# Two x tiles get space of their own, and the orders of all engines are drawn up anew

## The chip, the cores and the metric

The kernel runs on one core of one Trainium2 chip. The metric is the device time of one execution in microseconds. The kernel before takes 1588.69 us, the median of three runs (1588.14 to 1590.66).

## What is computed

One hybrid layer on x of 2048 rows and 1024 columns: RMSNorm, a combined input projection, a sliding-window attention with 16 query and 4 key heads of 64, a retention with 8 heads of values of 128, gates by SiLU, the output projection and the residual. Of the reference, cut to what matters:

```python
h = rms_norm(x, norm_gain)
proj = jnp.einsum('bsd,de->bse', h, w_in)
aq, ak, av, ag, rq, rk, rv, rg = jnp.split(proj, SPLIT_POINTS, axis=-1)
attn = window_attention(aq, ak, av, q_norm_gain, k_norm_gain, sink_logits)   # window 128, ALiBi, sinks
ret = retention(rq, rk, rv, ret_norm_gain)        # chunks of 64, state carried, group norm
mixed = jnp.concatenate([attn * jax.nn.silu(ag), ret * jax.nn.silu(rg)], axis=-1)
x = x + jnp.einsum('bse,ed->bsd', mixed, w_out)
```

## The kernel before

The sequence is cut into 4 blocks of 512 rows, the heads into 4 groups. A unit n is one block with one group, so there are 16 units, 0 to 15, and units 0 to 3 are the first block. A block has four x tiles of 128 rows, t = 0 to 3.

Every matmul is done in three: each operand is split into a high half (written by a copy to fp32r) and a low half (what is left), and high by high, high by low and low by high are added up. ScalarE (ACT) writes the high halves, GpSimd (POOL) the low halves of the weights, VectorE (DVE) those of x. In units 0 to 3 the weights are split on the chip and both halves saved to DRAM; later units load the halves.

TensorE (PE) works on jobs. Job(n, j) is one bank of 512 columns: j 0 to 3 are q, k and v of the four row tiles (weight panel 0 of the unit), 4 and 5 the attention gate, 6 and 7 the retention's q and k (panel 1), 8 to 11 its v and gate (panel 2), 12 to 19 the output projection (panel 3). The output jobs of unit n run within unit n + 1. Panels take turns in two buffers, wH and wL. Between the jobs stand the small operations of PE: TQ (transposes of the normalised q and k, L1453), S_ (scores, L1463), PT and PV (transposed probabilities, and their product with v), A, I and MT (retention), XB (the row scales, spread over a tile, L1553).

The first panels go as follows. load(q) (L312) brings a quarter of a panel, two of its eight k slices, to a staging slot; q 0 to 3 are panel (0,0), 4 to 7 panel (0,1), 8 to 11 panel (0,2). There are three slots, and q = 3 lies in sx, which is free at the start. wh1(n,p,s) (L520) on ACT writes the high half of slice s, wl1 (L382) on POOL the low half. A job that is first in its panel waits for each slice's low half (s_wl, L1434). x_turned(0,t) (L261) loads tile t of the transposed x to xt, which has two halves: tile 2 waits until the low halves of tile 0 are done (s_xL of 8), tile 3 those of tile 1. xh (L706) and xl (L1149) write the high and low half of tile t, in four pieces of two slices, to hTH and hTL. Jobs 0 to 3 need the slices of their own tile only, jobs 4 to 7 those of all four. xsq sums the squares of a tile of x rows, xms_ and xpow make the row scale from them; qkv(0,t) on ACT takes the bank of job(0,t) and that scale, qk_stats and qk_norm on DVE (L927, L938) normalise it, with rpow on POOL between them.

On DVE, carry_in(0) (L908) waits for the attention constants, part1 and part2 (L964, L990) are the softmax of a tile, ptl and mix take probabilities and result further, kw_am, kwl_al, rvg, rupd and gna to gnb belong to the retention. The pair qn lies in the same space as obt, which mix uses.

All DMAs go out from SyncE (SP), in its order. It waits in order too: an instruction that waits holds all those behind it. save(q) (L213) stores a quarter of a split panel.

Every engine has its order written out as calls, unit by unit (POOL L434 to L515, ACT L718 to L885, DVE L1157 on, PE L1564 to L1674). Dependencies are semaphores. The head of SP's order, of DVE's and of PE's stand in the diff.

Of the kernel before, what the change touches and what calls it, by code (L numbers as in the profile page):

```python
# [94 lines left out]
def build(nc, x, norm_gain, q_gain, k_gain, sinks, ret_gain, xT, wp0, wp1, wp2, wp3, c_bias, c_ret, c_ident, out):  # L95
# [9 lines left out]
    with ExitStack() as ctx:  # L105
# [272 lines left out]
        def _(pool):  # L378
# [62 lines left out]
            ggm(0, 0); wl1(1, 0, 3); ggm(0, 1); wl1(1, 0, 4); mixl(0, 2); wl1(1, 0, 5); wl1(1, 0, 6)
            wl1(1, 0, 7); mixl(0, 3); gpow(0, 0); ggm(0, 2); wl1(0, 3, 0); wl1(0, 3, 1); wl1(0, 3, 2)
            wl1(0, 3, 3); gpow(0, 1); ggm(0, 3); wl1(0, 3, 4)

            rpow(1, 0); wl1(0, 3, 5); wl1(0, 3, 6); wl1(0, 3, 7); gpow(0, 2); rpow(1, 1); rpow(1, 2)
            wl1(1, 1, 0); gpow(0, 3); wl1(1, 1, 1); wl1(1, 1, 2); rpow(1, 3); wl1(1, 1, 3); wl1(1, 1, 4)
            wl1(1, 1, 5); wl1(1, 1, 6); wl1(1, 1, 7); wl1(1, 2, 0); wl1(1, 2, 1); wl1(1, 2, 2); wl1(1, 2, 3)
            wl1(1, 2, 4); wl1(1, 2, 5); wl1(1, 2, 6); wl1(1, 2, 7); mixl(1, 0); rql(1); mixl(1, 1); rkl(1)
            wl1(2, 0, 0); wl1(2, 0, 1); wl1(2, 0, 2); mixl(1, 2); wl1(2, 0, 3); ggm(1, 0); wl1(2, 0, 4)
            wl1(2, 0, 5); wl1(2, 0, 6); wl1(2, 0, 7); ggm(1, 1); mixl(1, 3); gpow(1, 0); ggm(1, 2); wl1(1, 3, 0)  # L450
            wl1(1, 3, 1); wl1(1, 3, 2); wl1(1, 3, 3); wl1(1, 3, 4); ggm(1, 3); gpow(1, 1); wl1(1, 3, 5)

            rpow(2, 0); wl1(1, 3, 6); rpow(2, 1); wl1(1, 3, 7); gpow(1, 2); rpow(2, 2); wl1(2, 1, 0)
# [1277 lines left out]
```

## Time and profile before

| | before |
|---|---|
| median of three runs | 1588.69 us |
| the profiled execution | 1589.65 us |
| its span | 1587.9 us |
| mean granted TensorE clock | 0.998 |
| PE busy | 1560.4 us, 98% |
| DVE, ACT, POOL busy | 1113.1, 853.2, 451.4 us |
| share of PE in the chain that ended last | 84% |

The profile is of one execution. Busy times say how long an engine had an instruction in work; matmuls overlap, so that a busy PE isn't PE at its peak. The wait of an engine is named by what released it.

### The profile page before, as it was taken

What the parts mean: (1) busy time and instruction counts of PE and PEld (TensorE: products, weight loads), DVE (VectorE), ACT (ScalarE), POOL (GpSimd) and SP (SyncE); (2) the same over time, 40 slices, a digit from 0 to 9 for tenths busy, and PEclk for the clock granted to TensorE, in tenths of its full rate; (3) what the DMA queues carried; (4) which work ended last, traced back from release to release, by engine and by line L of the source; (5) the groups of instructions that cost most, each with busy time, mean ns of one, the idle gap of its engine ahead of it and who ended that gap; (6) DMA issues with size and microseconds to landing.
All of it is one profiled execution on the core that took longest, in us unless ns stands there. A gap on an engine that the chain in (4) does not pass through costs nothing.

```text
span 1587.9 us, 24908 instructions
## 1 busy us (share of the span) xinstructions
PE 1560.4 (98%) x8120; PEld 1354.2 (85%) x8120; DVE 1113.1 (70%) x2934; ACT 853.2 (54%) x2421; POOL 451.4 (28%) x453
## 2 busy tenths in 40 slices
...
GB/s 260 330 315 280 175 345 186 285 208 178 323 256 166 188 146 188 186 209 145 186 215 225 247 128 195 205 99 247 168 159 282 148 197 189 149 179 156 154 207 54
DMA packets 123328, 323.66 MB, mean 204 GB/s; under 512 B 16832, under 2 KB 60224, under 8 KB 123200
## 3 DMA queue, kind: packets, MB, share of 16 engines
...
## 4 chain that ended last, share of the span: by engine, by line
PE 84%; DVE 9%; issue 3%; ACT 2%; DMA 1%; POOL 1%; SPq 0%; DVEq 0%; POOLq 0%; ACTq 0%
PE jb L1441 24%; PE jb L1443 24%; PE jb L1442 24%; PE ob L1500 2%; PE s L1476 2%; PE ptb L1485 2%; PE ob L1460 1%; PE s L1539 1%; DMA stage<-wp_dram 1%; PE s L1538 1%; DVE hTL L1153 1%; PE ab L1550 1%; DVE acc L1139 1%; PE s L1377 1%; DVE qS L955 1%
## 5 line engine op out<-in xcount | busy, mean ns | idle before, releaser
L1441 PE MATMUL jb<-wH,hTH 128*128 128x512 f32 (+1 forms) x1024 | 376.6, 368 | 9.4 <-POOL wL L387 9.4
L1442 PE MATMUL jb<-wL,hTH 128*128 128x512 f32 (+1 forms) x1024 | 372.6, 364 | 0.0
L1443 PE MATMUL jb<-wH,hTL 128*128 128x512 f32 (+1 forms) x1024 | 372.3, 364 | 0.0
L1441 PEld LDWEIGHTS jb<-wH,hTH 128*128 128x128 f32 x1024 | 193.3, 189 | 30.0 <-POOL wL L387 11.9
L1443 PEld LDWEIGHTS jb<-wH,hTL 128*128 128x128 f32 x1024 | 193.3, 189 | 20.5
L1442 PEld LDWEIGHTS jb<-wL,hTH 128*128 128x128 f32 x1024 | 193.7, 189 | 17.6
L1441 PE MATMUL jb<-wH,mxH 128*128 128x512 f32 x512 | 207.6, 405 | 0.0
L1441 PE MATMUL jb<-hTH,wH 128*128 128x512 f32 x512 | 202.7, 396 | 2.8 <-POOL wL L387 2.8
L1443 PE MATMUL jb<-wH,mxL 128*128 128x512 f32 x512 | 200.6, 392 | 0.0
L1442 PE MATMUL jb<-wL,mxH 128*128 128x512 f32 x512 | 200.3, 391 | 0.0
L1442 PE MATMUL jb<-hTL,wH 128*128 128x512 f32 x512 | 199.7, 390 | 0.0
L1443 PE MATMUL jb<-hTH,wL 128*128 128x512 f32 x512 | 199.5, 390 | 0.0
L589 ACT ACTIVATE sx<-sx,nm 128x128 f32<-128x128 f32 x256 | 99.9, 391 | 160.9 <-DVE d L988 160.7
L412 POOL TENSOR_TENSOR mxL<-mixr,mxH 128x256 fp32r<-128x256 f32 x64 | 47.8, 747 | 465.4 <-ACT mxH L651 464.3
L387 POOL TENSOR_TENSOR wL<-stage,wH 128x512 fp32r<-128x512 f32 (+1 forms) x126 | 156.5, 1265 | 68.3 <-ACT wH L531 68.0
L1441 PEld LDWEIGHTS jb<-hTH,wH 128*128 128x128 f32 x512 | 96.2, 188 | 22.9 <-POOL wL L387 4.5
L1443 PEld LDWEIGHTS jb<-wH,mxL 128*128 128x128 f32 x512 | 96.1, 188 | 21.0
L1443 PEld LDWEIGHTS jb<-hTH,wL 128*128 128x128 f32 x512 | 96.1, 188 | 20.7
L1442 PEld LDWEIGHTS jb<-hTL,wH 128*128 128x128 f32 x512 | 96.3, 188 | 18.1
L1442 PEld LDWEIGHTS jb<-wL,mxH 128*128 128x128 f32 x512 | 96.6, 189 | 16.5
L1441 PEld LDWEIGHTS jb<-wH,mxH 128*128 128x128 f32 x512 | 96.3, 188 | 16.5
L394 POOL TENSOR_TENSOR rstd<-ms,mhalf 128x5 f32<-128x5 f32 x64 | 75.9, 1186 | 113.6 <-DVE ms L932 113.5
...
## 6 DMA issues: line engine op xcount, KB each, us to landing
...
```

What stands on the lines that cost most here:

```text
L387: pool.tensor_tensor(wL[b][:, s, 0:w], stage_of(at // 2, w)[:, s % 2], wH[b][:, s, 0:w].bitcast(F32), ALU.subtract).then_inc(S["s_wl"], 1)
L394: pool.tensor_tensor(rstd[:, t % 2], ms[:, t % 2], mhalf[:, 0:5], ALU.pow).then_inc(S["s_rstd"], 1)
L412: pool.tensor_tensor(mxL[:, 0:2, cols], mixr[:, :, :], mxH[:, 0:2, cols].bitcast(F32), ALU.subtract).then_inc(S["s_mixl"], 1)
L589: act.activation(v, v, ACT.Exp, bias=nm4[:, t % 2, i:i + 1], accum_out=den[:, t % 2, i:i + 1])
L955: v.scalar_tensor_tensor(out=qS[other, t % 2, :, a * 64:a * 64 + 64], in0=tr[rows, 0:256].rearrange("p (c q) -> p c q", q=64), scalar=qkg[ ...
L1139: v.tensor_tensor(a, a, bank_of(n, J_OUT + i)[:, :], ALU.add).then_inc(S["s_acc"], 1)
L1441: pe.matmul(o, lh, rh_, start=i == 0, stop=False)
L1442: pe.matmul(o, lh, rl_, start=False, stop=False)
L1443: m = pe.matmul(o, ll, rh_, start=False, stop=i == last)
L1476: m = pe.matmul(s_parts[:, par, hp], qS[:, t % 2, 2 * hp + par], kHL[:, :, win], start=True, stop=True)
L1485: m = pe.transpose(ptb[:, i * P:(i + 1) * P], sx[:, at:at + P], ident[:, :])
L1500: m = pe.matmul(o, v, pT[:, par * 256:(par + 1) * 256].rearrange("p (r q) -> p r q", q=64), start=i == 0, stop=i == 1)
```

## The change

A tensor xt23, two tiles of x in size, is declared in the space that mxL takes afterwards (mxL is now declared ahead of mxH, so that the two spaces are the same). Tiles 2 and 3 of the first block are loaded there, with no wait, with two semaphores of their own; ACT's and DVE's splits of them read from there. The condition for load(6) becomes that slot 0 is free of q = 0 (2 low halves, not 8). On SP, loads 6 and 4 go ahead of x tile 3, of the gains and of the attention constants, and load 5 ahead of the x rows of tile 2. qk_norm of the first two tiles of a unit waits until mix of the unit before has ended.

The orders of POOL, ACT, DVE and PE are new in all 16 units; much in units 0 to 4, by neighbours that change places in most others. In unit 0, PE has jobs 0 to 3 with nothing between them, TQ(0,0) behind job 4 and S_(0,0) behind job 5, and PV(0,3) goes to unit 1. ACT has the high halves of x tile 3 and four weight slices of panel 1 ahead of qkv(0,0); DVE has half of the low halves of x tile 3 behind qk_stats(0,0). From unit 5 on PE has "job(n,1); job(n,2); I(n-1,3)" everywhere. The core of the diff:

```diff
-        mxH, mxL = sb("mxH", [P, 4, BLK], F32R), sb("mxL", [P, 4, BLK], F32R)
+        with nc.sbuf_tensor("xt23", [P, 2, KT, P], F32) as xt23:
+            pass
+        mxL, mxH = sb("mxL", [P, 4, BLK], F32R), sb("mxH", [P, 4, BLK], F32R)
...
+        def x_tile(b, t):
+            return xt23[:, t - 2] if b == 0 and t >= 2 else xt[:, t % 2]
...
-                if t >= 2:
+                if b and t >= 2:
                     sp.wait_ge(S["s_xL"], 32 * b + 8 * (t - 1))
                 elif b:
                     sp.wait_ge(S["s_xsq"], nth(b, 4, t + 2))
-                sp.dma_start(xt[:, t % 2], xT[b, t]).then_inc(s_xt[t % 2], 16)
+                landed = s_xu[t % 2] if b == 0 and t >= 2 else s_xt[t % 2]
+                sp.dma_start(x_tile(b, t), xT[b, t]).then_inc(landed, 16)
...
-                if q >= STAGES + 1:
-                    sp.wait_ge(S["s_wl"], 2 * (q - STAGES) + 2)
+                if q > STAGES:
+                    sp.wait_ge(S["s_wl"], 2 * (0 if q == 6 else q - STAGES) + 2)
...
             first_rows(1)
+            load(6)
+            load(4)
             x_turned(0, 3)
             qk_gains()
             attention_constants(0)
-            load(4)
+            load(5)
             first_rows(2)
-            load(5)
             first_rows(3)
-            load(6)
             load(7)
...
+            xh(0, 0, 0); wh1(0, 0, 0); wh1(0, 0, 1); wh1(0, 0, 2); wh1(0, 0, 3); xh(0, 0, 1); wh1(0, 0, 4)
+            wh1(0, 0, 5); xh(0, 0, 2); wh1(0, 0, 6); wh1(0, 0, 7); xh(0, 0, 3); xh(0, 1, 0); xh(0, 1, 1)
+            xh(0, 1, 2); xh(0, 1, 3); xsq(0, 0); xh(0, 2, 0); xh(0, 2, 1); xh(0, 2, 2); xh(0, 2, 3); xsq(0, 1)
+            wh1(0, 1, 0); wh1(0, 1, 1); xh(0, 3, 0); xh(0, 3, 1); xh(0, 3, 2); xh(0, 3, 3); wh1(0, 1, 2)
+            wh1(0, 1, 3)
+
+            qkv(0, 0); wh1(0, 1, 4); wh1(0, 1, 5); xsq(0, 2); wh1(0, 1, 6); xsq(0, 3); qkv(0, 1); wh1(0, 1, 7)
+            xrb_copy(0); v_shift(0, 0); qkv(0, 2); v_shift(0, 1); qkv(0, 3); v_shift(0, 2); tqh(0, 0)
+            wh1(0, 2, 0); wh1(0, 2, 1); ag(0, 0); wh1(0, 2, 2); v_shift(0, 3); tqh(0, 1); wh1(0, 2, 3); ag(0, 1)
...
+                elif n:
+                    v.wait_ge(S["s_mixr"], 4 * n)
                 v.wait_ge(S["s_rstd"], nth(n, 4, t))
...
-            xms_(0, 0); xl(0, 1, 3); xl(0, 2, 0); xl(0, 2, 1); xl(0, 2, 2); xms_(0, 1); xl(0, 2, 3)
+            xl(0, 1, 3); xl(0, 2, 0); xl(0, 2, 1); xl(0, 2, 2); xms_(0, 0); xl(0, 2, 3); xms_(0, 1); carry_in(0)
+            xl(0, 3, 0); xl(0, 3, 1)
...
+            qk_stats(0, 0); xms_(0, 2); xl(0, 3, 2); xms_(0, 3); xl(0, 3, 3); qk_norm(0, 0); qk_stats(0, 1)
+            v_parts(0, 0); v_parts(0, 1); qk_norm(0, 1); qk_stats(0, 2); v_parts(0, 2); agz(0, 0)
+            qk_stats(0, 3); qk_norm(0, 2); tql(0, 0); agg(0, 0); v_parts(0, 3); agz(0, 1); qk_norm(0, 3)
+            tql(0, 1); agg(0, 1); part1(0, 0); rl(0, 0); rq_decay(0); tql(0, 2); part1(0, 1); part2(0, 0)
...
-            job(0, 0); job(0, 1); job(0, 2); TQ(0, 0); job(0, 3); S_(0, 0); job(0, 4); TQ(0, 1); XB(0)
-            job(0, 5); S_(0, 1); TQ(0, 2); job(0, 6); S_(0, 2); TQ(0, 3); PT(0, 0); job(0, 7); S_(0, 3)
-            PV(0, 0); PT(0, 1); job(0, 8); PV(0, 1); PT(0, 2); A(0, 0); job(0, 9); PV(0, 2); PT(0, 3); A(0, 1)
-            job(0, 10); PV(0, 3); I(0, 0); A(0, 2); job(0, 11); I(0, 1); A(0, 3)
+            job(0, 0); job(0, 1); job(0, 2); job(0, 3); XB(0); job(0, 4); TQ(0, 0); job(0, 5); TQ(0, 1)
+            S_(0, 0); job(0, 6); TQ(0, 2); S_(0, 1); job(0, 7); TQ(0, 3); S_(0, 2); job(0, 8); PT(0, 0); A(0, 0)
+            job(0, 9); PT(0, 1); S_(0, 3); PV(0, 0); A(0, 1); job(0, 10); I(0, 0); PT(0, 2); PV(0, 1); A(0, 2)
+            job(0, 11); I(0, 1); PT(0, 3); PV(0, 2); A(0, 3)
...
-            job(9, 0); I(8, 2); MT(8, 0); job(9, 1); I(8, 3); job(9, 2); TQ(9, 0); MT(8, 1); job(9, 3)
+            job(9, 0); I(8, 2); MT(8, 0); job(9, 1); job(9, 2); I(8, 3); TQ(9, 0); MT(8, 1); job(9, 3)
...
-            job(15, 0); I(14, 2); MT(14, 0); job(15, 1); I(14, 3); MT(14, 1); job(15, 2); TQ(15, 0); job(15, 3)
+            job(15, 0); I(14, 2); MT(14, 0); job(15, 1); job(15, 2); MT(14, 1); I(14, 3); TQ(15, 0); job(15, 3)
```

## Rows read from the trace of the kernel before

**Rows 1.** The page: busy us of PE, its share, its instructions.

```profile
PE 1560.4 (98%) x8120; PEld 1354.2 (85%) x8120; DVE 1113.1 (70%) x2934; ACT 853.2 (54%) x2421; POOL 451.4 (28%) x453
```

**Rows 2.** Table by stretches: busy us (count) of each engine, clock, DMA share, GB/s.

```profile
16.00:24.30 8.30, 8.30 (x49) 8.00 (x47) 4.36 (x20) 6.92 (x21) 2.76 (x3) 1.00 0.44 141
24.30:27.00 2.70, 0.42 (x3) 0.40 (x3) 1.55 (x9) 0.00 (x0) 0.00 (x0) 0.90 0.94 329
27.00:33.30 6.30, 6.29 (x31) 5.97 (x30) 3.24 (x13) 6.00 (x13) 5.11 (x5) 0.77 0.90 318
33.30:43.00 9.70, 6.90 (x29) 4.45 (x28) 9.17 (x20) 8.49 (x26) 9.14 (x8) 1.00 1.04 391
```

**Rows 3.** PE's waits, 0 to 100 us (total, times, longest), then its timeline.

```profile
PE jb L1441 <- POOL wL L387: 12.2, 9, 8.1
PE ob L1460 <- DVE rawqn L946: 2.3, 1, 2.3
PE ob L1500 <- DVE mixr L1028: 1.2, 1, 1.2
PE s L1476 <- DVE kHL L960: 1.0, 1, 1.0
...
32.83 0.74 PE L1476 MATMUL s<-kHL,qS 128*128 128x256 f32 x4
33.40 0.39 PE L1441 MATMUL jb<-hTH,wH 128*128 128x512 f32 x1
...
49.05 0.64 PE L1476 MATMUL s<-kHL,qS 128*128 128x256 f32 x4
...
96.69 0.34 PE L1441 MATMUL jb<-wH,hTH 128*128 128x384 f32 x1
```

**Rows 4.** Timelines of SP's queue, DVE and ACT: start, length, what, [idle before].

```profile
13.30 0.33 SPq L267 DMA_DIRECT2D xt<-xT_dram  x1
17.09 0.33 SPq L267 DMA_DIRECT2D xt<-xT_dram  x1
21.94 0.59 SPq L317 DMA_DIRECT2D stage<-wp_dram  x1
31.44 0.82 SPq L218 DMA_DIRECT2D scrH<-wH  x1
...
25.45 0.17 DVE L915 TENSOR_SCALAR nsink<-sink 128x2 f32<-128x2 f32 x1 [3.74 <-DMA sink<-sink_logits_dram]
...
27.19 1.15 ACT L531 ACTIVATE wH<-stage 128x512 fp32r<-128x512 f32 x2 [3.71 <-DMA stage<-wp_dram]
```

**Rows 5.** Timelines of POOL and DVE.

```profile
7.06 6.06 POOL L387 TENSOR_TENSOR wL<-stage,wH 128x384 fp32r<-128x384 f32 x6 [6.22 <-ACT wH L531]
...
73.86 1.20 POOL L412 TENSOR_TENSOR mxL<-mixr,mxH 128x256 fp32r<-128x256 f32 x1 [2.63 <-ACT mxH L651]
...
7.65 8.71 DVE L1153 SCALAR_TENSOR_TENSOR hTL<-xt,ngain,hTH 128x128 fp32r<-128x128 f32 x12 [1.43 <-ACT hTH L715]
...
16.46 2.31 DVE L1153 SCALAR_TENSOR_TENSOR hTL<-xt,ngain,hTH 128x128 fp32r<-128x128 f32 x8
```

**Rows 6.** The stretch from 33.3 to 97 us, and DVE's timeline.

```profile
33.30:97.00 63.70, 57.72 (x292) 46.69 (x291) 53.60 (x111) 42.23 (x118) 40.47 (x37) 1.00 0.90 325
...
37.04 1.30 DVE L986 SCALAR_TENSOR_TENSOR nm<-m,nsink 128x4 f32<-128x4 f32 x1
```

**Rows 7.** PE's waits from 100 to 1500 us, and from 1500 us to the end.

```profile
PE s L1538 <- issue: 2.2, 9, 0.3
PE ob L1460 <- DVE kHL L960: 1.7, 3, 0.7
PE ob L1500 <- DVE pTL L899: 0.8, 2, 0.6
PE ob L1500 <- DVE mixr L1028: 0.5, 1, 0.5
...
PE s L1538 <- DVE kwL L899: 1.1, 1, 1.1
```

More of the change, by code:

```diff
@@ L441, in _ @@
[L441 to L453, printed above, removed]
@@ new lines, in _ @@
+            gnm(0, 3); tql(1, 0); qk_stats(1, 3); gnb(0, 3); v_parts(1, 2); add(0, 0); qk_norm(1, 3); mtl(0, 2)
+            tql(1, 1); add(0, 1); v_parts(1, 3); add(0, 2); rl(1, 0); add(0, 3); tql(1, 2); mtl(0, 3)
+            part1(1, 0); add(0, 4); part1(1, 1); add(0, 5); tql(1, 3); add(0, 6); part2(1, 0); add(0, 7)
+            part2(1, 1); carry_out(1); agz(1, 0); part1(1, 2); ptl(1, 0); agg(1, 0); agz(1, 1); part2(1, 2)
+            ptl(1, 1); agg(1, 1); part1(1, 3); mix(1, 0); rq_decay(1); part2(1, 3); mix(1, 1); ptl(1, 2)
@@ new lines, in _ @@
+            qk_stats(2, 1); gnm(1, 2); v_parts(2, 1); gnb(1, 2); qk_norm(2, 1); gna(1, 3); gnv(1, 3)
+            qk_stats(2, 2); v_parts(2, 2); gnm(1, 3); mtl(1, 1); qk_norm(2, 2); gnb(1, 3); tql(2, 0)
+            qk_stats(2, 3); add(1, 0); v_parts(2, 3); add(1, 1); qk_norm(2, 3); mtl(1, 2); tql(2, 1); add(1, 2)
+            part1(2, 0); add(1, 3); tql(2, 2); mtl(1, 3); rl(2, 0); part1(2, 1); add(1, 4); part2(2, 0)
+            add(1, 5); xms_(1, 0); xms_(1, 1); xms_(1, 2); part2(2, 1); ptl(2, 0); tql(2, 3); add(1, 6)
@@ L1252, in _ @@
+            qk_stats(7, 2); v_parts(7, 2); tql(7, 0); gna(6, 3); gnv(6, 3); qk_norm(7, 2); mtl(6, 1); gnm(6, 3)
+            qk_stats(7, 3); v_parts(7, 3); gnb(6, 3); qk_norm(7, 3); add(6, 0); tql(7, 1); rl(7, 0); add(6, 1)
             part1(7, 0); mtl(6, 2); add(6, 2); part2(7, 0); tql(7, 2); part1(7, 1); add(6, 3); mtl(6, 3)
@@ L1293, in _ @@
-            tql(10, 3); ptl(10, 0); add(9, 5); carry_out(10); add(9, 6); part1(10, 2); add(9, 7); part2(10, 2)
+            kw_am(9, 0); kwl_al(9, 0); rvg(9, 1); kw_am(9, 1); rupd(9, 0); gna(9, 0); kwl_al(9, 1); rl(9, 1)
+            mix(9, 3); gnv(9, 0); gnm(9, 0); kw_am(9, 2); rvg(9, 2); gnb(9, 0); kwl_al(9, 2); rupd(9, 1)
+            gna(9, 1); gnv(9, 1); rl(9, 2); gnm(9, 1); carry_in(10); gnb(9, 1); kw_am(9, 3); rvg(9, 3)
+            rupd(9, 2)
+            qk_stats(10, 0); v_parts(10, 0); gna(9, 2); rl(9, 3); qk_norm(10, 0); kwl_al(9, 3); gnv(9, 2)
```

779 lines of the change are left out of this document (384 added, 395 removed).

## Prediction, made before the changed kernel ran

> **What bounds the kernel now.** I read first the page's totals [rows 1]: TensorE (PE) is busy for 1560.4 of 1587.9 us, so the change can only win what PE doesn't do now: 27.5 us. Then the table by stretches [rows 2] shows where these lie. From 16.0 to 24.3 us PE is full. From 24.3 to 27.0 it works 0.42 of 2.7 us, and the granted clock, 1.00 before, is 0.90 there and 0.77 until 33.3: a mean of its two levels, 2.4 and 1.2 GHz, so 46% of those 6.3 us are at the lower one. From 33.3 to 43.0 it works 6.90 of 9.7 us.
>
> Next what PE waited for in its first 100 us, and its timeline there [rows 3]. The reader is to see four things. POOL's low halves of the weights cost 12.2 us in nine waits, 8.1 of them before the first matmul, which stay; most of the rest stands in job(0,4), the first that needs panel 1: it goes from 33.40 to 42.8 us, where job(0,5), behind TQ and XB, has 5.5 us for the same 24 matmuls until 49.05. TQ(0,0), the transposes of the first normalised q, comes 2.3 us late. S_(0,2) waits 1.0 and PV(0,1) 1.2 us. Job(1,0) starts at 96.69, which I use as the mark for the end of unit 0.
>
> Why they come late is in the other engines' rows [rows 4]. SyncE's queue (SP) holds x tile 2 until 13.30 and x tile 3 until 17.09, because each waits that half of xt is free. Four gain loads and three of the attention constants follow, each 0.56 to 0.66 us of issue. The panel's first load goes out at 21.94. DVE waits 3.74 us for the sink, and qk_norm(0,0) stands behind that. ACT waits 3.71 us for the panel's first piece, until 27.19.
>
> **The change, part by part.** Sums are made on the profiled execution: 1589.65 us, its span of 1587.9 and 1.75 around it. The median is 1588.69, so I take off 0.96 at the end.
>
> *x tiles 2 and 3 in the space of mxL.* Nothing is added: the same two loads, without their waits. Tile 2 goes out behind the first rows, near 7 us rather than 13.30; tile 3 behind two weight loads. mxL is first written by mixl(0,0), at 73.86 before [rows 5]; hTL's last read of x is near 30 us, so this costs nothing. If tile 2 crowds the first panel's last piece, there is cover: POOL comes to that piece only at 7.06 + 6.06 = 13.1 us [rows 5], and ACT needs some 1 us for it.
>
> *Loads 6 and 4 ahead of x tile 3, constants and gains.* Load 6 waits for POOL's second low half only, load 4 for the fourth. POOL does six in 6.06 us from 7.06 [rows 5], 1.01 each, so they go out near 9.2 and 11.2 us. A load lands 5.2 us after its issue when the queue is idle (21.94 to 27.19 [rows 4]), so load 4 lands near 17.5, ten microseconds earlier. Behind the wait of load 4 on SP stand x tile 3, the four gains (2.4 us) and the constants (1.9 us): tile 3 goes out near 11.7, lands near 19, the sink at 20.5 rather than 25.4, load 5 out at 16.5.
>
> *PE's new order in unit 0.* All of jobs 0 to 3 come first, then XB, job 4, and TQ(0,0) only there. So the stop of 2.3 us goes, and its slow matmuls: 46% of 6.3 us at half the clock [rows 2] did the work of 1.45 us, so 1.5 us. But job(0,3) needs hTL of tile 3, and DVE's new order puts qk_stats(0,0) and two sums of squares between its pieces. I follow ACT: from 12.8 us its sixteen scalings of tiles 1 and 2 at 0.31 and two squares at 1.05 end at 19.8, two weight pieces at 20.9, tile 3 at 23.4, two more pieces 24.5, qkv(0,0) 25.9, two pieces and xsq(0,2) 28.0, a piece and xsq(0,3) 29.6. DVE can give hTL for k 4 and 5 only at 28.7, for 6 and 7 at 30.3. Job(0,3) starts at 24.2, does half in 2.1 us, waits 2.4 and 1.1 us, and ends near 31.5, or 32.5 with POOL's work beside it. This is a new stop of 3.5 us, and as long as the old one, so it brings back a slow stretch: 1.2 us. Job(0,4) then starts near 33, as before, but with five of its eight low halves done: 5.5 us rather than 9.4. That removes 3.7 us.
>
> *DVE after that.* S_(0,0) comes behind job(0,5), near 45 us; before, it was at 32.83 [rows 3]. ag(0,0) on ACT stands behind a weight piece whose load (8) follows ten save transfers, at about 1.03 us each, and the two retention constants; these start 7 us earlier than the 31.44 of before [rows 4], so load 8 lands near 43 us and part1(0,0) starts near 49 us. From 33.3 to 97 DVE is busy 53.6 us [rows 6]; 9.9 us of that (statistics, norms, two tql, gates: 4 x 0.6, 4 x 0.55, 2 x 1.25 and so on) is done before part1. So 43.7 us remain from 49 us on. With the waits PE and ACT still cause it (I take 4 us) and 4 to 5 us of it that the new order leaves for unit 1 (ptl(0,3), mix(0,3) and the like), DVE lets PE go on to job(1,0) at 92 to 95 us; I take 93.5. On PE this shows as waits of some 3.5 us at S_(0,1), S_(0,2), A(0,0) and a PT. In sum for unit 0: gone are 2.3 + 1.5 + 3.7 + 1.0 + 1.2 (PV) + 1.65 (job(0,8) took 7.1 us, 5.45 without POOL's pacing) = 11.35; new are 3.5 + 1.2 + 3.5 = 8.2. Net -3.2 us, and 96.69 - 3.2 = 93.5 agrees. Bounds: -8 (job(0,3) never stops) and +7 (DVE stretched, below).
>
> Here the trace speaks against the change: DVE's twelve hTL operations beside POOL's run of subtractions took 8.71 us, 0.73 each, and eight without it 2.31, 0.29 each [rows 5]. The tiny nm took 1.30 us beside POOL's pieces [rows 6]. The Trainium skill, "SBUF — State Buffer", section "Who interferes with whom", says that a DVE instruction with two SBUF inputs contends with a GpSimd instruction that reads SBUF and waits for its whole length; the trace agrees (0.73 against 0.29 us), and by that rule every POOL piece that the change moves beside such work costs DVE up to one piece.
>
> *Units 1 to 4.* All orders are new. PE's waits for DVE from 100 to 1500 us are 1.7 + 0.8 + 0.5 = 3.0 us [rows 7], all but one of 0.7 in these four units. The new orders can gain those 2.3 and may lose as much as one such stop of 0.7 per unit, 2.8. No row tells which; I take -0.8.
>
> *Units 5 to 14.* The form job, I(n,3), job becomes job, job, I(n,3). Nine stops of 0.24 us, 2.2 in all, stand at I [rows 7]; eight are at the old form, which units 5, 8 and 12 don't have, and one at the new form in unit 8. Seven of the eight are in these units, 1.7 us. So I take -1.3; bounds -2.0 and +0.5. DVE and ACT orders here change by neighbours only and hide under PE, which is full.
>
> *The last unit.* 0.7 us at TQ(15,0) and 1.1 at an I [rows 7]. TQ moves back by a place; another I still waits for the same chain. I take 0, bounds -0.9 and +0.7. The new wait of qk_norm for mixr has mix(n-1,3) ahead of it on DVE itself, so it waits for nothing; the qk_stats behind it are untouched. If mix were late, TQ would be too, price one norm, 0.55 us.
>
> Sum: -3.2 - 0.8 - 1.3 = -5.3; 1589.65 - 5.3 = 1584.35, less 0.96 gives **1583.4 us**.
>
> **The rivals.** *Full gain.* Job(0,3) isn't held, because the squares come sooner than I have them. For it: x rows 0 and 1 land early. Against: ACT's list above has no slack. Then the 4.7 us of the new stop and slow clock go too, with DVE's start 4 us earlier: 1583.4 - 4.0 = 1579.4.
>
> *Given back.* PE leads by 4 us after job(0,4), and DVE, late by 12 us with its first scores, takes it back before job(1,0), or the new orders of units 1 to 4 lose 2 to 3 us. For it: DVE was busy 53.6 of 63.7 us there. Against: ten of those were idle and the new order defers mix(0,3). Unit 0 nets 0 and only the -1.3 stays: 1587.4, between 1585.6 and 1590.
>
> *Slower: DVE and POOL in each other's way.* Splits of panels 1 and 2 now run beside the squeezed attention work. POOL was busy for 40.47 of those 63.7 us [rows 6]. If ten more of DVE's two-input operations each lose 1.0 us (as nm's 1.30, for an operation on four columns), job(1,0) starts at 103.5, not 93.5, and 1583.4 + 10 = 1593.4. It decides from 3.2 + 5.3 = 8.5 us of such losses on.
>
> *It doesn't do what it says.* The early transfers slow the first panel or land no sooner, since SP waits at load 4. DMA engines were busy only 0.44 in 16 to 24.3 us [rows 2], which speaks against it: no gain at the start, 1587 to 1590.
>
> **How the numbers follow.** The forecast, 1581 to 1585.5, has 0.50; full gain 0.13; given back 0.25; slower 0.09; not done 0.03. Faster by over 0.2% (below 1585.5; 0.2% is about what a measurement of this kernel can tell from no change) is 0.50 + 0.13 + a sliver of given back = 0.64; within 0.2% 0.27; slower 0.09. The range is 1579.0 to 1589.5: it leaves out the slower case and the far end of the full gain.
>
> **What would show it.** Job(0,4) 5.5 us long, starting near 33; a stop in the second half of job(0,3) released by hTL; no TQ stop at 24 us; the sink landed by 21; S_(0,0) near 45; DVE almost without idle time from 49 us; job(1,0) at 92 to 95; fewer 0.24 us stops after 500 us. Wrong would make it: job(1,0) later than 96, or new stops of over 2 us in units 1 to 4.

## The result, and the profile after

The kernel after takes 1576.68 us (median, 1575.85 to 1578.02) against 1589.6 of the kernel before beside it: ratio 0.9918, 95% interval 0.9902 to 0.9934. The profiled executions have spans of 1575.1 and 1587.9 us. The forecast was 1583.4 us, with a range down to 1579.0: the direction was right, the time lies 2.3 us below the range, and the gain is 12.8 us of span rather than 5.3.

The page after (the line of totals, then the chain by engine) stands against [rows 1]. TensorE (PE) is busy 4.6 us less, and its idle time fell from 27.5 to 19.3 us:

```profile
PE 1555.8 (99%) x8120; PEld 1357.6 (86%) x8120; DVE 1119.0 (71%) x2934; ACT 851.1 (54%) x2421; POOL 450.9 (29%) x453
...
PE 91%; DVE 3%; DMA 2%; issue 1%; POOL 1%; ACT 1%; SPq 1%; ACTq 0%; POOLq 0%; DVEq 0%
```

PE's waits, first from 0 to 100 us (against [rows 3]), then 100 to 500 and 1450 to the end ([rows 7]; from 500 to 1450 us the view lists none, where before had eight):

```profile
PE jb L1456 <- POOL wL L394: 7.8, 1, 7.8
PE jb L1456 <- ACT rawqn L548: 2.7, 1, 2.7
PE s L1491 <- DVE sx L988: 1.9, 1, 1.9
PE jb L1456 <- DVE hTL L1165: 0.2, 1, 0.2
...
PE ab L1565 <- DVE mxL L909: 1.2, 2, 0.7
PE ob L1475 <- DVE kHL L972: 1.0, 1, 1.0
PE jb L1456 <- DVE acc L1151: 0.3, 1, 0.3
...
PE s L1553 <- DVE rst L909: 0.3, 1, 0.3
```

The table by stretches, as [rows 2], with 50 to 57 us added:

```profile
16.00:24.30 8.30, 8.10 (x47) 7.78 (x45) 3.85 (x22) 6.38 (x19) 3.87 (x4) 1.00 0.81 288
24.30:27.00 2.70, 0.22 (x1) 0.23 (x2) 1.06 (x5) 1.86 (x4) 1.19 (x1) 1.00 0.83 312
27.00:33.30 6.30, 6.30 (x29) 6.06 (x29) 4.07 (x16) 5.62 (x13) 6.01 (x7) 0.73 1.06 395
33.30:43.00 9.70, 9.70 (x46) 7.94 (x46) 6.18 (x16) 6.21 (x17) 6.49 (x6) 1.00 0.90 342
50.00:57.00 7.00, 5.13 (x21) 3.89 (x20) 6.69 (x15) 5.29 (x18) 4.15 (x3) 0.81 1.03 415
```

Where the time went is best read from the starts of the jobs, which I took one by one from PE's timeline. How much earlier than in the kernel before each starts, in us, for after and for the experiments below:

| kernel | job(0,5) | (1,0) | (2,0) | (6,0) | (15,0) | (15,19) |
|---|---|---|---|---|---|---|
| after | 4.5 | 5.1 | 1.5 | 5.6 | 10.1 | 12.7 |
| loads_alone | 2.5 | 2.6 | 2.6 | 3.2 | 2.6 | 2.7 |
| orders_alone | -1.9 | -3.7 | -7.2 | -2.9 | 1.6 | 4.2 |
| tail_new | 0.3 | 0.3 | 0.3 | -0.1 | 4.4 | 6.9 |
| pe_exchange | 0.5 | 0.5 | 0.5 | 1.3 | 1.8 | 1.8 |
| pe_exchange_rupd | -0.9 | -1.5 | -1.5 | -0.9 | 2.0 | 2.0 |
| ag_tqh_first | 5.2 | 7.1 | 2.0 | 5.9 | 10.4 | 13.0 |
| tql_first | 4.7 | 5.3 | 2.3 | 6.5 | 11.1 | 13.7 |
| both_first | 4.8 | 8.0 | 4.9 | 8.9 | 13.4 | 16.0 |

At job(6,0) both kernels have done the same work. At the marks in between they haven't: at job(0,5) after still has S_(0,0) and TQ(0,1) to do, it leaves PV(0,3) to unit 1, and does I(n,2) ahead of the next unit (1.27 us, job(5,0) to job(5,1)). So the gain has three parts: 5.6 us up to job(6,0), 4.5 in units 6 to 14, 2.6 in the last unit. The prediction had 4.0, 1.3 and 0.

These leads come from one profile of each kernel. Five kernels share the code of before up to job(1,0) (before, tail_new, pe_exchange, pe_exchange_rupd, kwl_first), and it starts there at 96.2 to 98.2 us; at job(6,0) those whose code is the same so far lie at 586.5 to 588.7, and after and after_again at 582.2 and 581.7. So a lead at an early mark is good to 1 or 2 us. Behind job(6,0) a unit whose orders are the same takes the same time to about 0.1 us in each profile, but for unit 12 (see below).

### The profile page after: what moved, and what is told of

The parts are those of the page before. It is cut to its first block, busy times and chain, and to the rows that moved or that the text cites. A ratio compares the mean times of both kernels' runs of the same rounds, so it can differ in the third digit from the quotient of the medians.

```text
span 1575.1 us, 24935 instructions
## 1 busy us (share of the span) xinstructions
PE 1555.8 (99%) x8120; PEld 1357.6 (86%) x8120; DVE 1119.0 (71%) x2934; ACT 851.1 (54%) x2421; POOL 450.9 (29%) x453
## 4 chain that ended last, share of the span: by engine, by line
PE 91%; DVE 3%; DMA 2%; issue 1%; POOL 1%; ACT 1%; SPq 1%; ACTq 0%; POOLq 0%; DVEq 0%
PE jb L1456 26%; PE jb L1457 26%; PE jb L1458 26%; PE s L1491 2%; PE ob L1515 2%; DMA stage<-wp_dram 2%; PE ptb L1500 2%; PE ob L1475 1%; PE s L1554 1%; PE ab L1565 1%; PE s L1553 1%; PE s L1392 1%; POOL wL L394 1%; PE ab L1392 0%; PE s L1394 0%
## 5 line engine op out<-in xcount | busy, mean ns | idle before, releaser
L1458 PEld LDWEIGHTS jb<-wH,hTL 128*128 128x128 f32 x1024 | 193.5, 189 | 20.5
```

Source lines behind the costliest of these rows:

```text
L1458: m = pe.matmul(o, ll, rh_, start=False, stop=i == last)
```

## The experiments

### Two halves of the change, and its tail alone

Theories: the early loads win unit 0 by themselves; the new orders do; or each needs the other. And for the units behind: their gain is their own, or it is left to them by the head.

loads_alone is the kernel after with the orders of the kernel before (POOL, ACT, DVE, PE); orders_alone is the kernel before with the orders of after and

```diff
+                elif n:
+                    v.wait_ge(S["s_mixr"], 4 * n)
```

in qk_norm; tail_new is the kernel before with the orders of after from unit 5 on. Edits of an order are shown here and below shortened to the calls that move and what stands between them.

> The space for x tiles 2 and 3, SP's order and the conditions of the loads as in the kernel after, the orders of ACT, DVE, POOL and PE as in the kernel before. Theory 1 (early weights are the gain of unit 0 and need no new order): the sink lands 2 to 5 us earlier, so the stop of TQ(0,0) goes or shrinks, and job(0,4) takes 5.5 to 7 rather than 9.4 us; job(1,0) at 91 to 93, total 4 to 5 us less, ratio 0.997. Theory 2 (DVE takes back what PE wins, unless the scores are put back as in the new order): job(0,4) shorter, but S_ and PV wait longer, job(1,0) at 95 to 97, ratio 0.999 to 1.000.

Measured: ratio 0.9988 (0.9977 to 0.9998). From the start of job(0,4), at 33.0 us, to that of job(0,5) it takes 7.9 us rather than 10.1. TQ(0,0) still stops, for 2.5 us. Nothing comes back: S_(0,2) and PV(0,1) stop for 1.0 and 1.2 us, as in before, and the 2.6 us of job(1,0) are still there at the end. So DVE does not take back what PE wins, as theory 2 had it, though the ratio is nearer to its 0.999 than to theory 1's 0.997; theory 1 was too generous by half.

> The other half: all orders of ACT, DVE, POOL and PE as in the kernel after, x tiles 2 and 3 in xt with their waits, and SP's order as in the kernel before. Before unit 1 the new ACT order has x tile 3 and four slices of panel 1 ahead of qkv(0,0); their load landed at 27.2 and the next behind it, so qkv(0,0) ends near 32 to 34 rather than 26.2, and job(0,3), which waits for its bank, starts 6 to 8 us later than after. Theory 1 (the loads and the order of unit 0 need each other): job(1,0) at 96 to 99, and with the 8.4 us of the units from 5 on still won, the total is 1581 to 1584, ratio 0.995 to 0.9965. Theory 2 (the order alone hides it, since DVE sets the end of unit 0 anyway): job(1,0) by 93, total as after, ratio 0.992.

Measured: ratio 0.9962 (0.9948 to 0.9975). Job(0,3) starts at 32.5 us. PE's timeline and ACT's in this kernel:

```profile
32.47 0.69 PE L1419 MATMUL jb<-wH,hTH 128*128 128x384 f32 x1 [8.19 <-ACT rawqn L534]
...
27.43 1.15 ACT L525 ACTIVATE wH<-stage 128x512 fp32r<-128x512 f32 x2 [5.61 <-DMA stage<-wp_dram]
28.49 2.43 ACT L709 ACTIVATE hTH<-xt,ngain 128x128 fp32r<-128x128 f32 x8
30.82 1.13 ACT L525 ACTIVATE wH<-stage 128x512 fp32r<-128x512 f32 x2
31.86 0.56 ACT L534 ACTIVATE rawqn<-jb,xr 128x384 f32<-128x384 f32 x1
```

The new order of ACT puts the weight slices ahead of qkv(0,0); with the late load it waits 5.61 us for the first, and PE waits 8.19 us for the bank. By job(6,0), where both have done the same work, the loads alone win 3.2 us, the orders alone lose 2.9, together they win 5.6: the order pays only on top of the loads, which is theory 1 (job(1,0) came at 100.4 us, though, not at 96 to 99). One more thing shows here. From job(1,0) to job(2,0) it takes 101.6 us, as in after, although unit 1 begins 8.7 us later; before and loads_alone take 98.0. So the new order makes unit 1 longer by 3.5 us whether PE comes early or late. Half of that is work moved into it, PV(0,3) (some 0.5 us) and I(1,2) (1.3); the rest, 1.8 us, are its stops.

> Units 0 to 4 and all loads as in the kernel before, the orders of all engines as in the kernel after from unit 5 on, the last unit among them. If the gains of the units simply add up, it wins what the two traces differ by behind job(5,0): 5.8 us by job(15,0) and 2.6 behind it, 8.4 in all, ratio 0.9947. By the terms of the prediction (units 5 to 14 -1.3, last unit 0) 1.3 us, ratio 0.9992. If the steady units ran faster only because of what the new head leaves them, it is within 1 us of before.

Measured: ratio 0.9947 (0.9933 to 0.9962). From job(6,0) to job(15,0) it wins 4.50 us, after wins 4.50, and behind job(15,0) both win 2.6. The tail's gain is its own. The ratio is the one expected, but the profile has 6.5 us rather than 8.4 behind job(5,0): the expectation had counted as gain the 1.27 us of I(4,2), which after does ahead of that mark, and unit 5 loses 0.5 us where the old orders meet the new.

### What a stop of 0.24 us costs

pe_exchange is the kernel before, with this in the PE order of units 6, 7, 9, 10, 11, 13 and 14 (here 9); pe_exchange_rupd adds the same kind of step on DVE and ACT:

```diff
-            job(9, 1); I(8, 3); job(9, 2)
+            job(9, 1); job(9, 2); I(8, 3)
```
```diff
-            rupd(8, 3); gnb(8, 2); qk_norm(9, 1)
+            gnb(8, 2); qk_norm(9, 1); rupd(8, 3)
-            rh(9, 0); qkv(9, 2); ocopy(8, 3); tqh(9, 0); mth(8, 1)
+            qkv(9, 2); ocopy(8, 3); tqh(9, 0); mth(8, 1); rh(9, 0)
```

> The kernel before, with one exchange in PE's order alone in units 6, 7, 9, 10, 11, 13 and 14: I(n-1,3) and job(n,2) change places, as after has them. All else, also DVE's and ACT's orders, is that of before. Theory 1 (a stop costs the gap between the starts of matmuls, some 0.5 us, of which the listed idle of 0.24 shows half): seven stops go, 3.5 us, ratio 0.9978, and job(15,0) starts 3 to 3.6 us earlier. Theory 2 (a stop costs its listed idle, as the prediction had it): 1.7 us, ratio 0.9989. Theory 3 (the gain of 0.5 us a unit in the kernel after comes from rupd, rh and rl that stand earlier on DVE and ACT, and PE's place does nothing): within 0.5 us of before.

Measured: ratio 0.9989 (0.9979 to 0.9999), the number of theory 2, but not for its reason. PE's timeline at I(8,3), in the kernel before and then in pe_exchange:

```profile
888.44 0.34 PE L1443 MATMUL jb<-wH,hTL 128*128 128x384 f32 x1
889.01 0.36 PE L1538 MATMUL s<-rst,zst 128*128 128x256 f32 x1 [0.23 <-issue]
889.21 0.28 PE L1539 MATMUL s<-rv,aH 128*128 128x256 f32 x1
...
890.97 0.33 PE L1443 MATMUL jb<-wH,hTL 128*128 128x384 f32 x1
891.14 0.28 PE L1538 MATMUL s<-rst,zst 128*128 128x256 f32 x1
891.26 0.28 PE L1539 MATMUL s<-rv,aH 128*128 128x256 f32 x1
```

Without a stop, I starts 0.17 us after the last matmul of the job starts; with it 0.57 us, and its own second matmul another 0.08 us later. So the stop costs 0.48 us, of which the view lists 0.23: the rest lies under the end of the matmul before. As a mean over units 9, 10, 11, 13 and 14, job(n,1) to job(n,3) takes 0.49 us less. But job(n-1,12) to job(n-1,13) takes 0.28 more, and the lead grows by 0.5 us only over nine units. Why, is seen in DVE's and ACT's timelines of pe_exchange:

```profile
892.39 0.71 DVE L1091 SCALAR_TENSOR_TENSOR rst<-rst,cret,s 64x128 f32<-64x128 f32 x2 [3.13 <-PE s L1379]
893.13 0.48 DVE L1119 SCALAR_TENSOR_TENSOR oraw<-oraw,xr,gg 128x256 f32<-128x256 f32 x1
893.53 0.48 DVE L943 TENSOR_TENSOR rawqn<-rawqn,rstd 128x320 f32<-128x320 f32 x1
...
893.13 1.27 ACT L673 ACTIVATE rst<-rst 64x128 fp32r<-64x128 f32 x4 [3.04 <-DVE rst L1091]
894.43 0.58 ACT L540 ACTIVATE rawqn<-jb,xr 128x384 f32<-128x384 f32 x1
```

DVE's rupd(8,3) waits for I(8,3), which now comes a job later, and qk_norm(9,1) stands behind it; ACT's rh(9,0) waits for rupd, and qkv(9,2) behind that. TQ(9,1) is late by what they lose.

> As pe_exchange (the kernel before, I(n-1,3) and job(n,2) exchanged on PE in seven units), and in the same units two steps that wait for I(n-1,3) moved back to where after has them: rupd(n-1,3) on DVE behind qk_norm(n,1), rh(n,0) on ACT behind mth(n-1,1). In pe_exchange DVE waited 3.1 us at rupd(8,3) and ACT 3.0 at rh(9,0), with qk_norm(9,1) and qkv(9,2) behind them, and job(n-1,12) grew by 0.28 us as TQ(n,1) came late. Theory 1 (a stop of 0.24 listed costs 0.49, and 0.28 of it came back through these two waits): all seven units keep 0.49, job(15,0) 3.4 us earlier than with the kernel before, ratio 0.9978. Theory 2 (TQ is late for another reason): as pe_exchange, job(n-1,12) to job(n-1,13) 3.29 us and not 3.01, 1.4 us in all.

Measured: ratio 0.9981 (0.9972 to 0.9989). In the same five units the 0.28 us are gone (3.01 us, as after) and the 0.49 stay. The lead from job(6,0) to job(15,0) grows by 2.9 us: 3.15 in the seven units, 0.2 in unit 8, less 0.4 in unit 12. Theory 1 holds for the seven units; the ratios of the two experiments alone would not tell them apart.

### The last unit

kwl_first is the kernel before with one edit on DVE, for t = 1 and 2 (the two stand in this order for t = 3 already):

```diff
-            rl(15, t); kwl_al(15, t)
+            kwl_al(15, t); rl(15, t)
```

> The kernel before with one edit: in unit 15 on DVE kwl_al(15,t) stands ahead of rl(15,t) for t = 1, 2, 3. I(15,t) waits for both, and rl waits 0.43 us for ACT's rh with kwl_al idle behind it. If that order makes the stop of I(15,2), 1.13 us listed and 1.34 from start to start, it shrinks to after's 0.30 and 0.46, and job(14,12) to job(14,13) takes 5.1 us rather than 5.97; total 0.9 us less, ratio 0.9994. If the stop came from the chain itself (as the prediction had it: another I waits for the same chain), 5.97 stays.

Measured: ratio 0.9994 (0.9985 to 1.0003), which the times alone can't tell from no change; job(14,12) to job(14,13) takes 5.28 us, against 5.97 before and 5.05 after. So three quarters of what that step gained is the order of two lines on DVE. PE's and DVE's timeline of the kernel before there:

```profile
1535.65 0.39 PE L1443 MATMUL jb<-wH,mxL 128*128 128x512 f32 x1
1537.16 0.36 PE L1538 MATMUL s<-rst,zst 128*128 128x256 f32 x1 [1.13 <-DVE kwL L899]
...
1535.60 0.59 DVE L899 TENSOR_TENSOR rst<-rst 64x128 fp32r<-64x128 f32 x2 [0.43 <-ACT rst L673]
1536.22 0.29 DVE L899 TENSOR_TENSOR kwL<-kwr,kwH 128x128 fp32r<-128x128 f32 x1
1536.43 0.42 DVE L899 TENSOR_TENSOR aL<-amr,aH 128x256 fp32r<-128x256 f32 x1
```

DVE waits 0.43 us for ACT with kwL and aL, which need nothing from it, behind; I needs all three.

This kernel showed something else, in unit 12, whose PE order is the same in all: PE stopped 1.36 us at I(11,3), where the kernel before had no stop. DVE's timeline, then PE's:

```profile
1177.30 0.17 DVE L915 TENSOR_SCALAR nsink<-sink 128x2 f32<-128x2 f32 x1 [3.30 <-DMA sink<-sink_logits_dram]
...
1185.50 0.36 PE L1529 MATMUL s<-rst,zst 128*128 128x256 f32 x1 [1.36 <-DVE kwL L899]
```

The old order of DVE has carry_in(12), which waits for a transfer, ahead of rupd(11,2). The new one has it behind qk_stats(12,1). How long DVE waits for that transfer goes with how long job(12,2) to job(12,3) takes: in before 1.60 us and 5.67; in loads_alone 1.70 and 0.41 more; in pe_exchange_rupd 2.07 and 0.39 more; in pe_exchange 2.23 and 0.55 more; in kwl_first 3.30 and 1.60 more. In after and tail_new, with the new order, it is 5.67. That this is why the runs of the kernel before spread wider (1588.4 to 1594.8 us beside after's 1575.6 to 1577.3 on one chip) is argued from the traces, not tried.

### The stops left in the head

Five kernels take the kernel after and move the stops of its first 50 us, a sixth takes work from DVE.

qkv_first, on ACT:

```diff
-            wh1(0, 1, 2); wh1(0, 1, 3); qkv(0, 0)
+            qkv(0, 0); wh1(0, 1, 2); wh1(0, 1, 3)
```

> The kernel after, with wh1(0,1,2) and wh1(0,1,3) behind qkv(0,0) on ACT, not ahead. It is the stop of job(0,3), 2.7 us, that is tried. Theory 1 (only the bank held it): qkv(0,0) ends at 23.0, job(0,3) runs through from 24.1 to 28.4 us, job(0,4) starts at 29 and is then paced by POOL, and job(0,5) starts 1 to 2 us earlier. Theory 2 (hTL of tile 3 holds it as well, as the prediction said, since on DVE xms_(0,2) with its sum of squares, at 29.4, stands ahead of it): job(0,3) starts at 24.1, stops inside for hTL until 29.7 and 31.2, and ends within 0.5 us of after's; total as after.

Measured: ratio 0.9915 (0.9902 to 0.9929), 1576.82 us. Job(0,3) starts at 24.7 us, stops inside for hTL (4.2 us in five waits) and job(0,4) starts at 32.67, after's 33.14. Theory 2: the stop that the prediction forecast is there, hidden in after behind the one at the bank.

start_free adds the low halves of x tile 3 ahead of carry_in(0) on DVE, and XB(0) behind job(0,4) on PE.

> As qkv_first, and the low halves of x tile 3 all ahead of carry_in(0) on DVE, XB(0) behind job(0,4) on PE. Nothing then holds job(0,3): it runs 24.1 to 28.4 us. Job(0,4) is paced by POOL's slices, 1.25 us each, the last of which stands behind three rpow and xpow, near 36 us. Theory 1: job(0,5) at 37 rather than 38.97, the slow clock of 27 to 33 us gone too, and the total 1.5 to 3 us less than after. Theory 2 (DVE sets the end of unit 0): job(0,5) at 37, but the stop at S_(0,1) grows from 1.9 by what was won, total as after within 0.5 us.

Measured: ratio 0.993 (0.9917 to 0.9942), 1579.81 us. Job(0,3) starts at 24.1 us and isn't held. But job(0,4) waits 3.23 us, until 31.67, for ACT to empty the bank of job(0,1), and job(0,5) 1.62 us, until 39.79, for that of job(0,2). The next jobs in the ring of three banks are held in turn; neither theory had it. That explains only a part: job(0,5) is 0.8 us behind after's, and the profiled execution is the fastest of five (1577.35 us). What makes the median 3 us slower than qkv_first's on the same chip stays open.

head_free frees that too: on ACT qkv(0,0), v_shift(0,0), qkv(0,1) stand ahead of the slices from 2 on, tqh(0,0), ag(0,0), tqh(0,1) ahead of wh1(0,2,0); on DVE and POOL the statistics and rpow follow. head_free_load8 has load 8 behind the third save besides.

> The kernel after with the first 50 us of ACT, DVE and POOL put in another order, so that none of the stops seen there is left to another: on ACT qkv(0,0) and qkv(0,1) right behind x tile 3 and ahead of the slices of load 5, tqh(0,0), ag(0,0) and tqh(0,1) ahead of the slices of loads 8 and 9; on DVE all low halves of x tile 3 ahead of the first statistics; on POOL rpow(0,0) and rpow(0,1) between the slices; on PE XB(0) behind job(0,4). Theory 1 (these stops were the limit): job(0,3) runs 24.1 to 28.4 us, job(0,4) is paced by POOL and ends at 35 to 36, job(0,5) starts 3 us earlier than after's 38.97, the stop at S_(0,1) is under 0.5 us, job(1,0) at 88 to 89, and the total 1.5 to 3 us less than after. Theory 2 (DVE sets job(2,0) in any case): job(1,0) at 88 to 90, job(2,0) within 0.7 us of after's 193.20, total within 0.7 us.

> As head_free, with load 8 on SP behind the third save, not behind the fifth and the retention's constants. It goes out near 29 rather than 36 us and lands at 37 to 39 rather than 43. By theory 1 nothing in the first 50 us waits for it in head_free any more, so this does nothing by itself (within 0.5 us of head_free), or costs up to 1 us where the slices of panel 2 on POOL move beside DVE's first softmax and stretch it.

Measured: ratios 0.9938 (0.9924 to 0.9952) and 0.9944 (0.9932 to 0.9957), 1580.4 and 1582.0 us: slower than after. Job(0,4) starts at 27.7 us, 5.4 us before after's, and job(0,5) at 41.3, 2.3 us behind it. The stretch of head_free:

```profile
34.00:43.00 9.00, 7.93 (x21) 5.51 (x21) 2.22 (x13) 4.91 (x12) 6.33 (x7) 0.50 0.90 319
```

The granted clock is 0.50 there, the lower level of 1.2 GHz throughout, where after has 1.00 from 33.3 to 43. PE came to job(0,4) before POOL's slices and waited for four of them between 30 and 38.5 us, 2.7 us in all; the clock fell behind the second, after 1.8 us of waits (0.89 in 30 to 34 us). But POOL's slices were late too. Its timeline at the last of panel 1, in head_free and then in after:

```profile
37.09 1.32 POOL L394 TENSOR_TENSOR wL<-stage,wH 128x512 fp32r<-128x512 f32 x1
...
32.37 3.85 POOL L394 TENSOR_TENSOR wL<-stage,wH 128x512 fp32r<-128x512 f32 x3
```

They end at 38.4 and 36.2 us: ACT's bank reads and POOL's own rpow now stand ahead of them. From the last slice to job(0,5) PE works 2.8 us at half the clock, so at the full one job(0,5) would start near 39.9 us (an estimate from these rows), still 0.9 behind after's 38.97. Of the 2.3 us some 1.4 are the clock and the rest POOL's order; no run holds PE back and leaves POOL's order as it is. The second kernel is slower than the first by 1.6 us, which is just what it loses between job(0,16) and job(0,17) in unit 1, to a stretch like the one shown for ag_tqh_first below.

ag_first moves ag(0,0) on ACT ahead of wh1(0,2,0).

> The kernel after, with ag(0,0) on ACT ahead of wh1(0,2,0), whose load lands at 42.95 us. DVE waited 1.94 us for ag(0,0) at 44.66, with part1(0,0) behind it, and S_(0,1) on PE waited 1.9 us for part1(0,0). Theory 1 (the late weight load is what stops S_(0,1)): agg(0,0) near 42.8, part1(0,0) 1.9 us earlier at 49.8, no stop at S_(0,1) and no slow clock behind it (0.81 in 50 to 57 us), job(0,8) 3 us earlier, of which unit 1 keeps at least half: total 1.5 to 3 us less than after. Theory 2 (DVE is full from there to unit 1 anyway): the stop goes, but the same time comes back by job(2,0), total within 0.5 us of after.

Measured: ratio 0.992 (0.9906 to 0.9933), 1577.6 us. DVE's wait for ag(0,0) is gone, but it waits 2.67 us for tqh(0,1), which stands behind the next weight load (landed at 45.8 us), and S_(0,1) still stops for 1.9 us. Theory 1 fell, since there were two loads ahead, not one; theory 2 fell in that the stop didn't go.

dve_light takes the kernel after and narrows the statistics and the gated product of unit 0's group norm and eight adds, so that its result leaves these parts out; one of the three edits:

```diff
-                    i = v.bn_stats(st[:, h], oraw[:, t % 2, h])
+                    i = v.bn_stats(st[:, h], oraw[:, t % 2, h] if n else oraw[:, t % 2, h, 0:16])
```

> The kernel after with less work for DVE between 95 and 145 us: for unit 0 alone the statistics and the gated product of the retention's group norm are taken over 16 of 128 columns of a head, and add(0,i) over 64 of 512 columns, so these parts of the result are left out. It takes some 0.3 us off each of eight operations and 0.5 off each of eight adds, 6 to 7 us in all. Theory 1 (DVE is full from job(1,0) to job(2,0), so what the head wins comes back there): the stops at ab, ob and jb there, 1.2 + 1.0 + 0.3 us, go, and job(2,0) starts 2.5 to 4 us earlier relative to job(1,0) than after's 101.56 us; the total is about 2.5 to 4 us less. Theory 2 (the stops there come from chains through ACT and POOL, not from DVE's load): job(1,0) to job(2,0) within 0.5 us of 101.56.

Measured: ratio 0.9907 (0.9893 to 0.992), 1575.98 us, not told from after's. DVE is busy 133.9 us from 20 to 195 us rather than 140.6, and job(1,0) to job(2,0) takes 100.5 us rather than 101.6. The stop of 1.0 us at ob is still there, that at ab is 0.3 us rather than 0.5, that of 0.3 at the add is gone. Of 6.7 us of work taken away 1.0 arrives, between the two theories: DVE's load makes the smaller part of the stops of unit 1.

### Order in unit 0 and in unit 1, apart and together

after_again is the kernel after on the same chip. ag_tqh_first, on ACT:

```diff
-            wh1(0, 2, 0); wh1(0, 2, 1); ag(0, 0); wh1(0, 2, 2); v_shift(0, 3); tqh(0, 1); wh1(0, 2, 3)
+            ag(0, 0); v_shift(0, 3); tqh(0, 1); wh1(0, 2, 0); wh1(0, 2, 1); wh1(0, 2, 2); wh1(0, 2, 3)
```

tql_first, on DVE and then ACT:

```diff
-            qk_norm(1, 3); mtl(0, 2); tql(1, 1)
+            tql(1, 1); mtl(0, 2); qk_norm(1, 3)
-            xsq(1, 0); tqh(1, 1)
+            tqh(1, 1); xsq(1, 0)
```

both_first has both edits.

> The kernel after once more, unchanged, as the measure for the three others on the same chip. Expected: 1576 to 1578 us, job(1,0) at 91 to 92 and job(2,0) at 193, unless the landing of load 5 moves job(0,3) as it did from 26.8 to 25.7 us in ag_first and dve_light.

Measured: 1576.44 us (1575.64 to 1577.26), ratio 0.9908 (0.9891 to 0.9926).

> The kernel after, with ag(0,0), v_shift(0,3) and tqh(0,1) on ACT ahead of wh1(0,2,0), so that neither stands behind loads 8 and 9. In ag_first, with ag(0,0) alone moved, DVE waited 2.67 us for tqh(0,1), and S_(0,1) still stopped for 1.9 us. Theory 1 (the two weight loads make that stop): part1(0,0) starts 2 to 2.5 us earlier than after's 51.7 us, S_(0,1) stops for under 0.3 us, no slow clock from 50 to 57 us; job(0,8) to job(0,9) as after; job(1,0) 2 to 3 us earlier, job(2,0) 1 to 2.5. Theory 2 (DVE's own work in 44 to 52 us makes it): part1(0,0) within 0.7 us, the stop stays near 1.9.

Measured: 1575.95 us (1575.33 to 1576.72), ratio 0.9907 (0.9892 to 0.9922). Part1(0,0) starts at 49.4 us, and the stretch from 50 to 57 us has

```profile
50.00:57.00 7.00, 6.72 (x34) 5.42 (x33) 6.71 (x12) 4.95 (x16) 4.34 (x4) 1.00 1.02 399
```

PE works 6.72 us at a clock of 1.00, where after has 5.13 at 0.81. Of the stop at S_(0,1) 0.28 us is left, but S_(0,2) now stops for 0.59 and A(0,0) for 0.85. Job(1,0) starts 2.1 us earlier than after's; but at job(2,0) 0.4 us is left. The 1.6 us are lost in one place, between job(0,16) and job(0,17), 4.45 us rather than 2.86. It is not that DVE takes the lead back: PE stops in unit 1 for the same 0.3, 0.5 and 1.0 us as in after (the last at 124.66, in after at 126.73). What differs is the granted clock. The stretch from 120 to 130 us in after, in ag_tqh_first, and in both_first below:

```profile
120.00:130.00 10.00, 8.20 (x40) 6.10 (x39) 9.50 (x17) 8.52 (x21) 8.34 (x7) 1.00 0.91 314
120.00:130.00 10.00, 8.49 (x31) 6.28 (x31) 9.78 (x17) 6.44 (x17) 6.42 (x5) 0.83 0.94 365
120.00:130.00 10.00, 8.60 (x44) 6.97 (x43) 9.76 (x18) 5.60 (x15) 5.57 (x5) 1.00 0.94 364
```

A mean of 0.83 over 10 us is 3.4 us at the lower level, at half the speed 1.7 us of work, which is what is missing. Qkv_first and head_free_load8 have the same 4.45 us there, all others that have after's PE order 2.9.

> The kernel after, with tql(1,1) and mtl(0,2) on DVE ahead of qk_norm(1,3) rather than behind it, and tqh(1,1) on ACT ahead of xsq(1,0). In after qk_norm(1,3) waits 0.39 us for POOL and then takes 1.52 + 1.32 us beside POOL's pieces, and TQ(1,2) stops for 0.97 and a MT for 0.55 us behind it. Theory 1 (order makes the stops of unit 1, not load): both go, job(1,0) to job(2,0) takes 99.6 to 100.2 rather than 101.56 us, and the total is 1.3 to 1.9 us less. Theory 2 (load): they turn up at TQ(1,3) or at a job's add, 101.56 stays within 0.4.

Measured: 1576.0 us (1575.18 to 1578.23), ratio 0.9907 (0.9891 to 0.9923). The stop at ob is gone, but a later add (acc) stops PE for 1.4 us: job(1,0) to job(2,0) takes 101.1 us rather than 101.56. This is what theory 2 (load) said, a stop that turns up elsewhere, at a job's add. With dve_light it leaves both: order and load make these stops together.

> The edits of ag_tqh_first and tql_first together. If both are order and add up: job(2,0) 2.5 to 4 us earlier than in after, total 1573 to 1574.5 us. If what unit 0 wins comes back in unit 1: no better than the better of the two.

Measured: 1573.97 us (1573.66 to 1575.34), ratio 0.9897 (0.988 to 0.9914). No execution of it is as slow as the fastest of after_again. By its leads at job(1,0), (2,0) and the end, 8.0, 4.9 and 16.0, unit 0 keeps what it wins. Each edit alone is worth 0.4 to 0.5 us, which its runs don't tell from nothing, both 2.5. The rows above say why that is more than the sum: with the stop at ob gone the clock stays at 1.00 in unit 1, and the 1.6 us that ag_tqh_first loses there are kept. This kernel beats before and after.

## Why the prediction fell short

The profile has 12.7 us where 5.3 were forecast. Of the 7.4 us between them 3.2 are in units 5 to 14, 2.6 in the last unit and 1.6 in units 0 to 5.

*Units 5 to 14: the size of a term.* The mechanism was right: the exchange removes the stops at I(n,3). I priced them by the idle time that the view lists, 0.24 us, and they cost 0.49 each, measured from start to start. Seven units and the new-form stop of unit 8 (0.52, and 0.31 at its job(7,12)) give 4.3 us; 0.25 at job(11,12) makes it 4.5, where the term was 1.3 and its bound 2.0. I also wrote that DVE's and ACT's orders "change by neighbours only and hide under PE". They don't hide: without them the exchange keeps only 0.2 us of its 0.49 (pe_exchange). Of a step that is moved on PE I had not asked who waits for it.

*The last unit: a term put at nothing.* I took 0, as "another I still waits for the same chain". The chain had 0.43 us of ACT in it with DVE idle, which the new order fills; kwl_first shows 0.69 us for that alone. And 0.71 us listed at TQ(15,0) was 0.87 from start to start (1479.55 to 1480.59 us, less 0.17). With the other stops it makes the 2.6 us.

*Unit 0: right places, two wrong reasons.* As forecast: load 6 and 4 out at 8.7 to 11.0 us (9.2 and 11.2), x tile 3 at 11.06 (11.7), load 5 at 16.02 (16.5), job(0,4) starts at 33.14 (33) and takes 5.6 us (5.5), S_(0,0) at 44.81 (45), load 8 landed by 42.95 (43), TQ(0,0) and PV without a stop. Wrong: load 5 took 9.1 us and the sink landed at 23.9 us, not 20.5. I had taken 5.2 us for a load from an idle queue, but the change has more transfers under way there: the DMA share from 16 to 24.3 us is 0.81, where before had 0.44 [rows 2]. So ACT waits 2.72 us for load 5:

```profile
25.11 1.15 ACT L539 ACTIVATE wH<-stage 128x512 fp32r<-128x512 f32 x2 [2.72 <-DMA stage<-wp_dram]
26.16 0.56 ACT L548 ACTIVATE rawqn<-jb,xr 128x384 f32<-128x384 f32 x1
...
26.78 0.53 PE L1456 MATMUL jb<-wH,hTH 128*128 128x384 f32 x1 [2.68 <-ACT rawqn L548]
```

and job(0,3) stops before it starts, for the bank that qkv(0,0) empties. There are three banks (L183), so a job waits for the reader of the third job before it. This wait is in the code and I had not listed it. The stop for hTL was real but hidden behind it (qkv_first); both together cost what I had for one: job(0,3) ended at 32.8, forecast 31.5 to 32.5. The slow clock (0.73 in 27 to 33.3 us) came as forecast. (The working took 3.7 us off for job(0,4); 9.4 less 5.5 is 3.9.)

*DVE behind the scores.* I forecast 3.5 us of waits at S_(0,1), S_(0,2), A(0,0) and a PT. Only S_(0,1) stopped, 1.9 us and a stretch at 0.81 of the clock, and most of it was ACT's order: ag_tqh_first moves nothing else and leaves 0.28 us of it. In that kernel two more of the forecast places, S_(0,2) and A(0,0), stop after all, for 0.59 and 0.85 us. DVE and POOL did hinder each other a little more: DVE was busy 1119.0 us against 1113.1 in all, with the same instructions. The slower rival, with its 10 us in unit 0, didn't come; where DVE ran beside POOL the stretched rows are there, 1.52 and 1.32 us for the norm of tile 3 in unit 1 (alone 0.49 and 0.22).

*Units 1 to 4 and "given back".* The rival's second half came: stops of 1.0, 0.5 and 0.3 us in unit 1 and one of 0.7 at ab at 413 us, in unit 4's stretch. Its first half, DVE taking back a lead, is not what the runs show. Unit 1 takes 101.6 us in after and in orders_alone, where PE comes 8.7 us later, and what ag_tqh_first loses in it is a slow clock behind the same stops. The net of units 0 to 5 was 5.6 us, not 0. With the moved work put at 0.5 us for PV(0,3) and 1.3 for I (an estimate from their rows), after leads by 4.6 us at job(1,0), 2.8 at job(2,0) and 5.6 at job(5,0): unit 0 won more than the 3.2 that I had, unit 1 lost 1.8, and units 2 to 4 won 2.8, where four stops of before (0.6, 0.5, 0.6 and 0.4 us) are gone; the prediction had 0.8 for units 1 to 4 together. Which moves there did it no run shows.

The range failed at its lower end since the stops of units 5 to 14 and of the last unit were priced by the same view, the listed idle time, and so were short together.
